# Low parts of eight weight chunks made by accumulating DMA instead of VectorE subtraction

## The reference, cut to what matters

```python
def merge_branches(attn, u, g, w_attn_out, dw_w, dw_b, ln_g, ln_b, w_conv_out, w_out):
    y_a = attn @ w_attn_out
    y_b = conformer_conv(u, dw_w, dw_b, ln_g, ln_b, w_conv_out)
    g_a, g_b = jnp.split(g, 2, axis=-1)
    return (jax.nn.sigmoid(g_a) * y_a + jax.nn.sigmoid(g_b) * y_b) @ w_out
...
    x = x + g1 * mix_x
    hx2 = modulate(rms_norm(x, norm2_g[i]), sh2, sc2)
    x = x + g2 * conv_glu_ffn(hx2, w_up[i], ffn_dw_w[i], ffn_dw_b[i], w_down[i])
```

## Time and profile before

| | |
|---|---|
| time, median of 3 runs | 968.76 us (968.25 to 969.23) |
| span of the profiled execution | 967.1 us |
| TensorE busy | 954.8 us (99%) |
| TensorE weight loads | 818.8 us (85%) |
| VectorE busy | 703.0 us (73%) |
| ScalarE busy | 490.7 us (51%) |
| GpSimd busy | 53.3 us (6%) |
| HBM traffic | 196 GB/s over the span |

### The profile page before, as it was taken

How to read it: one execution, slowest core, us unless ns; L and a number is a source line. 1 busy time by engine, 2 the same in 40 slices (tenths; PEclk the granted TensorE clock), 3 DMA queues, 4 the chain that set the end, 5 groups by cost and what they waited for, 6 DMA issues and landing times.

```text
span 967.1 us, 14404 instructions
## 1 busy us (share of the span) xinstructions
PE 954.8 (99%) x5644; PEld 818.8 (85%) x5644; DVE 703.0 (73%) x912; ACT 490.7 (51%) x650; POOL 53.3 (6%) x90
## 2 busy tenths in 40 slices
PE   8999999999999999999999999999999999999997
PEld 5798788888988888889888888898988888888885
DVE  3589998579879999758776763474656977775455
ACT  3574565864465555325445433248855644444342
POOL 0241000000000000010000000001101000000000
PEclk9999999999999999999999999999999999999999
DMA  9954353665476655943665555173522565555511
GB/s 373 400 225 172 134 215 132 234 241 192 182 264 216 216 180 209 333 170 124 249 241 213 178 213 195 66 285 133 192 100 87 215 232 184 190 201 194 197 44 44
DMA packets 27987, 190.13 MB, mean 197 GB/s; under 512 B 3136, under 2 KB 3520, under 8 KB 5920
## 3 DMA queue, kind: packets, MB, share of 16 engines
q1 hardware_dynamic: 26336, 184.23, 51.6%
q0 software_dynamic: 1456, 5.12, 1.7%
q10 hardware_dynamic: 144, 0.07, 0.0%
HBM read 188.35 MB, written 1.05 MB: 196 GB/s over the span
## 4 chain that ended last, share of the span: by engine, by line
PE 92%; DMA 3%; ACT 2%; issue 1%; DVE 1%; SPq 0%; POOL 0%; POOLq 0%; DVEq 0%; ACTq 0%
PE acc L1160 23%; PE acc L1163 11%; PE acc L700 10%; PE acc L702 10%; PE acc L701 10%; PE acc L703 4%; PE acc L705 4%; PE acc L704 4%; DMA early<-in_early 3%; PE acc L847 3%; PE acc L1104 2%; PE acc L1032 1%; PE acc L1011 1%; PE acc L1135 1%; PE acc L1107 1%
## 5 line engine op out<-in xcount | busy, mean ns | idle before, releaser
L1943 DVE TENSOR_TENSOR wlo<-raw,whi 128x2048 fp32r<-128x2048 f32 (+1 forms) x140 | 316.3, 2266 | 141.7 <-ACT whi L1443 141.6
L1443 ACT CAST whi<-raw 128x2048 fp32r<-128x2048 f32 (+1 forms) x144 | 270.4, 1889 | 141.3 <-PE acc L702 92.9
L1160 PE MATMUL acc<-x_parts,whi 128*128 128x512 f32 x960 | 301.5, 395 | 0.0
L1163 PEld LDWEIGHTS acc<-x_parts,wlo 128*128 128x128 f32 x960 | 180.3, 188 | 42.6
L1163 PE MATMUL acc<-x_parts,wlo 128*128 128x256 f32 x960 | 188.6, 278 | 0.0
L1160 PEld LDWEIGHTS acc<-x_parts,whi 128*128 128x128 f32 x960 | 146.1, 189 | 0.0
L700 PE MATMUL acc<-whi,h_hi 128*128 128x512 f32 x264 | 103.0, 390 | 0.0
L702 PE MATMUL acc<-whi,h_lo 128*128 128x512 f32 x264 | 102.7, 389 | 0.0
L701 PE MATMUL acc<-wlo,h_hi 128*128 128x512 f32 x264 | 102.7, 389 | 0.0
L703 PE MATMUL acc<-x_parts,whi 128*128 128x256 f32 x312 | 90.3, 289 | 0.0
L705 PE MATMUL acc<-x_parts,wlo 128*128 128x256 f32 x312 | 88.3, 283 | 0.0
(11 more groups left out here) (314 smaller groups left out, 1200.2 us busy)
## 6 DMA issues: line engine op xcount, KB each, us to landing
raw<-in_stream SPq DMA_DIRECT2D x164, 1024.0 KB, 4.8
early<-in_early SPq DMA_DIRECT2D x8, 1024.0 KB, 15.1
X<-in_x SPq DMA_DIRECT2D x2, 512.0 KB, 4.6
G<-in_ctx SPq DMA_DIRECT2D x1, 1024.0 KB, 22.0
bc<-in_g_ffn_post POOLq DMA_DIRECT2D x2, 512.0 KB, 4.9
MX<-in_bias POOLq DMA_DIRECT2D x1, 1024.0 KB, 6.4
out<-X SPq DMA_DIRECT2D x4, 256.0 KB, 2.1
bc<-in_c_row POOLq DMA_DIRECT2D x1, 512.0 KB, 4.7
```

The source lines that it names most:

```text
L1160: pe.matmul(acc[:, BANK[i + q] + o, :], w[0][:, k, o * P:(o + 1) * P], xs[:, k, :], start=(k == 0), stop=False)
L1163: mm = pe.matmul(acc[:, BANK[i + q] + o, T:2 * T], w[1][:, k, o * P:(o + 1) * P], xhi[:, k, :], start=False, stop=(k == KD - 1))
L1443: act.copy(of_split(whi[si_slot], si), of_split(raw[raw_slot], si)).then_inc(s["hi_done"], 1)
L1943: dve.tensor_tensor(of_split(wlo[slot], si), of_split(raw[raw_slot], si), of_split(whi[slot], si), ALU.subtract).then_inc(s["lo_done"], 1)
```

## The change

The low parts of eight chunks, a0 to a3 and w0 to w3, are no longer made by VectorE. ScalarE first writes the negated high part into `wlo` (a copy of `raw` with scale -1, rounded to fp32r), then the high part into `whi`. When `hi_done` has counted the chunk, GpSimd issues a transfer from `raw` (in SBUF) to `wlo` (in SBUF) that adds to what stands there: -high + raw is the low part. Its landing raises one of four new semaphores, `low_in0` to `low_in3`, by buffer. `low_ready(si)` gives the semaphore and value that tell that split number si is ready: for the eight chunks the new one, for all others `lo_done`, whose count is 8 lower behind them. TensorE's `chunk_ready`, SyncE's `slot_free` and the loops of `up` use it. GpSimd's eight waits and issues stand before `norm(2)`. The semaphore `x6_half`, on which nothing waits, is removed.

```diff
+BY_DMA = range(SPLIT["attnout0"], SPLIT["wout"] + 4)
+
+
+def low_ready(si):
+
+    before = min(max(si - BY_DMA.start, 0), len(BY_DMA))
+    if si in BY_DMA:
+        return f"low_in{si % NR}", 16 * (before // NR + 1)
+    return "lo_done", si + 1 - before
...
-                kind.append(("lo_done", SPLIT[name] + j - WHOLE.get(name, 0) + 1))
+                kind.append(low_ready(SPLIT[name] + j - WHOLE.get(name, 0)))
...
-                        sp.wait_ge(s["lo_done"], SPLIT[name] + 2 - WHOLE.get(name, 0) + 4 * m + q + 1)
+                        sp.wait_ge(s["lo_done"], low_ready(SPLIT[name] + 2 - WHOLE.get(name, 0) + q)[1] + 4 * m)
...
             load_gain("final_g", 2)
+            for si in BY_DMA:
+                pool.wait_ge(s["hi_done"], si + 1)
+                pool.dma_start(wlo[si % NR][:, :], raw[chunk_of[si] % NR][:, :], accum_op=ALU.add)\
+                    .then_inc(s[f"low_in{si % NR}"], 16)
             norm(2)
...
             def chunk_ready(n):
-                pe.wait_ge(s["lo_done"], n + 1)
+                sem, value = low_ready(n)
+                pe.wait_ge(s[sem], value)
...
-                    pe.wait_ge(s["lo_done"], si + 4 * m + q + 1)
+                    pe.wait_ge(s["lo_done"], low_ready(si + q)[1] + 4 * m)
...
+                if si is not None and si in BY_DMA:
+                    act.activation(wlo[si_slot][:, :], raw[raw_slot][:, :], ACT.Copy, scale=-1.0)
                 act.copy(of_split(whi[si_slot], si), of_split(raw[raw_slot], si)).then_inc(s["hi_done"], 1)
...
-                    split(si % NR, chunk_of[si] % NR, si + 1, si)
+                    if si not in BY_DMA:
+                        split(si % NR, chunk_of[si] % NR, si + 1, si)
                     n_split[0] += 1
...
-                x6_lo(k, slice(0, P)).then_inc(s["x6_half"], 1)
+                x6_lo(k, slice(0, P))
```

More of the change, by code:

```diff
@@ L305 @@
     SOURCE[f"down{_n}"] = [wide(_name, 2 * r) for r in range(11)]
-SEMS = """hi_done lo_done mod_used mod_dot c_in c_sig c_row mod_row mod_ps chunk_used acc_ready const_in rest_in vec_in x_in0 x_in1 ctx_in p_in gain_in table_in
+SEMS = """hi_done lo_done low_in0 low_in1 low_in2 low_in3 mod_used mod_dot c_in c_sig c_row mod_row mod_ps chunk_used acc_ready const_in rest_in vec_in x_in0 x_in1 ctx_in p_in gain_in table_in
 sct_zero silu_c moda_ps xt_in xt_act x0 q_used x0_hi x0_lo mod_out affine1 tables
-ss_ready ri_ready xn_ready xn_half x6_half bt_act bt_dve xf_act xf_dve bx_hi bx_lo xt_ps shift_dve xhi xlo
+ss_ready ri_ready xn_ready xn_half bt_act bt_dve xf_act xf_dve bx_hi bx_lo xt_ps shift_dve xhi xlo
 q_ss v_done q_ri q_norm q_rot q_tps q_t
```

## The result

The changed kernel takes 1006.79 us (median of 4 runs, 1001.21 to 1008.43) against 968.94 (968.25 to 969.23) beside it: ratio 1.0383, 95% interval 1.0368 to 1.0398, so +37.8 us. The profiled execution is the quickest of the four, 1001.21 us with a span of 999.4; what follows explains its +32.3. A second set of runs of the same kernel gave 1002.97 (1001.39 to 1009.44; ratio 1.0369, 1.0330 to 1.0409). The runs differ among themselves by 8 us, those of before by 1.

A forecast was written before the change was run, and what follows sets the result against it. TensorE alone was taken to set the time, without idle time from 198 to 262. VectorE's freed time gave 0; stalls at the attention and output chunks summed to 26.2 us: 968.8 + 26.2 = 995, range 977 to 1016.

The forecast's parts named there:

- likeliest case: Accumulates at a0 to w3 hold the engines 3.5 to 6 us: 17 to 35 us slower, 986 to 1004, chance 0.55.
- the walk: Chunk-by-chunk timeline from a0 to w3 of transfers, held loads and splits: stalls summing to 26.2 us.
- Value of VectorE's freed time, 0: Eight subtractions removed from VectorE, 18 us in all, gain nothing because TensorE has no idle time there.
- ScalarE's second pass, 1.88 us, and w3 late by 0.9: Each negated copy takes ScalarE 1.88 us; w3's high part comes 0.9 us later than TensorE's need.
- Places and sum of the stalls: TensorE stalls at a1, a2, a3 and w0 to w3, 0.2 to 7.3 us each, sum 26.2.
- E = 5, F = 3: Per accumulating transfer: E, holding the 16 DMA engines, 5 us; F, the rest of its time alone, 3.0 us.
- Rival 1: Each transfer costs the DMA engines no more than a load, 2.46 us: 978 to 981 us, chance 0.23.
- Rival 2: The transfer's add or fp32r conversion is slow, 7.5 to 10 us: 46 to 66 us of stalls, 1015 to 1035, chance 0.14.
- With the two queues sharing the engines evenly: Transfers and loads split the DMA engines evenly when both have work; an assumption behind the 26.2 us sum.
- The check by capacity: From 190, eight transfers and ten loads need 64.6 us of engines: w3's low part at 256.6 at no idle.
- Rival 3: TensorE's clock halves behind stalls of 5 to 7 us: +3 to +8 us on top of the sum; no separate chance.
- Rival 4: Not slower: at w3 the loss stays within 1.9 us only if the accumulate lands in 1.0 us; chance 0.03.

The follow-up runs named there:

- neg_only: Kernel before the change with ScalarE's eight negated copies added, VectorE still subtracting and no transfer: 972.72 us, +3.9 (1.0041).
- copy_not_add: Changed kernel with a plain copy in place of each accumulating transfer, so the low parts are wrong: 984.84 us, +16.0 (1.0172).
- hold_back: Changed kernel with the last scale2 load, the first of up0 and those behind them waiting for w3's low part: 998.37 us (1.0311).
- a0_only: Changed kernel with only a0's low part made by the transfer: 969.23 us against 968.81 for the kernel before (1.0005).
- half: Changed kernel with transfer and negated copy on 1024 of 2048 columns of each chunk, VectorE subtracting the other 1024: 983.88 us, +15.1 (1.0151).

## Why the prediction was nearly right, step by step

The forecast was 995, in a range of 977 to 1016. 1006.79 lies within it, but above the likeliest case (986 to 1004), and +37.8 is more than the +26.2 and the 17 to 35 given for it; the second set, 1002.97, lies inside both. In the profiled execution w3 starts 30.2 us later than before (267.14 against 236.96), where the walk had 26.2, and 2.1 more are lost behind it.

- **Value of VectorE's freed time, 0.** Held: 18 us less busy, and TensorE never waited for it before but for 0.17 us.
- **ScalarE's second pass, 1.88 us, and w3 late by 0.9.** Held: 1.90 to 1.95 us each; in neg_only w3's high part ends at 237.95, as forecast (237.8). Alone the copies cost +3.9, nearly all of it through the later high and low part of w3.
- **Places and sum of the stalls.** The sum is 25.6 against 26.2, but that is luck. In the order a1, a2, a3, w0, w1, w2, w3 the walk had 5.1, 0.2, 2.0, 1.9, 7.3, 4.9 and 4.8; measured were 6.83, 0, 0, 4.24, 7.17, 1.41 and 5.96. Only w1 is near, a2 and a3 are no stalls, and the sum ran against a TensorE that I took to be at full clock. By the chain, which does not depend on TensorE, w3's low part came at 267.1, not at 263.1.
- **E = 5, F = 3.** Measured 5.4 and 1.9; against the copy's 2.7 us that is twice, and by the median packets, 629 : 325, 1.9 times. The rule of the Trainium skill that the prediction weighed ("Collectives: The Full Stack", section "The bandwidth ceiling: the fold count and why AG ≠ RS ≠ AR": an add needs two source reads and runs at half a copy's rate) has this ratio right. Rival 1 (E = 2.46) is out: copy_not_add shows where that would have ended, at +16, not at +9 to +12. Rival 2 (E = 7.5 to 10) is out by the same 5.4.
- **"With the two queues sharing the engines evenly": the step that failed.** They take turns by packet, and an accumulated packet is twice as long. From a0's issue to w3's low part the walk had 77.0 us: transfers 41.7 (9.3, 9.2, 11.6, 11.6), loads 23.9 (7.1, 7.1, 9.7), ScalarE's splits 11.4. Measured: transfers 36.2, loads 32.9 (8.15, 12.56, 12.17), the rest 12.5; together 81.6. The transfers were 5.5 too long in the walk and the loads 9.0 too short. Of the 12.56 us of w0's load 4.4 pass before its first packet, while a2's transfer goes on (1.0 for the load issued at 195.77 on free engines), 7.4 in turns with the transfers (8 x 0.938 = 7.5), and 0.7 behind the last packet. w3's load has 4.1 and 7.1, at first behind scale2.2's load in its own queue too.
- **The check by capacity.** As it stood it gave 256.6, further from 267.1 than the walk. It counted too little: from 190 to 267 GpSimd's queue held the engines for 55.2% of 77 us, 42.5 us, and the loads for 41.8%, 32.2 us, where it had 40 and 24.6. With these, 190 + 74.7 + 2 = 266.7; among the loads it left out are those that hold_back put off.
- **Rival 3, the clock.** Not a rival but a term of the sum: 7.3 us of the 32.9 lie in slow stretches, 2.1 of them behind w3 where nothing absorbs them, less than the +3 to +8 named there. I had forecast 26.2 without it, and had put a granted clock below 1.00 in 215 to 290 among the signs of being wrong: it was 0.82 from 204 to 267. Even the 2.2 us wait of neg_only brought the clock down.
- **Rival 4, landing in 1.0 us.** Out: the quickest landing of an accumulate of 1 MB was 6.94.
- **Not explained:** 5.6 us between the profiled execution and the median, and why runs spread by 8 us where transfers set the pace. No run gives the loads buffers of their own, so how much of the loss is the held loads and how much the full engines is read from the chain alone.

None of the kernels beats the one before. TensorE has no idle time in 198 to 262, so a version can at best be equal, as a0_only is.

## What to carry over

Work may be moved to an engine with a longer latency where the cover is longer than the latency, chunk by chunk: a0, wanted some 19 us after its issue, was free; w3, wanted at once, paid all. Before moving it, follow what the source buffer held longer delays, since the loads behind it cost as much as the operation. And count a shared DMA engine by packets and their durations, not by even shares, and allow for the wait before the first packet: a load had 1.0 us on free engines, and six of half's eight transfers 3.5 to 5.2 us beside other traffic.

## What was not expected of the hardware

- An accumulate from SBUF to SBUF holds a DMA engine for 629 ns for 8 KB, a plain copy for 325, a load from HBM for 309; smaller packets do worse by the byte (178 ns for 2 KB).
- Halving the bytes of the transfers brought their median landing only from 10.1 to 8.5 us.
- GpSimd's issue takes 0.84 to 0.95 us for an accumulate and 0.53 us for the copy of the same size.
- TensorE's granted clock fell to 0.50 after a wait of 2.2 us, and came back within five microseconds.
